# The experts' down product in high and low parts, with all outgoing rows copied by ScalarE

## The chip, the cores and the metric

The kernel runs on one core of one Trainium2 chip. The metric is the device time of one launch in microseconds (us), the median of several runs. The engines named below are TensorE (PE; PEld is its loading of the stationary operand), VectorE (DVE), ScalarE (ACT), GpSimd (POOL), which issues the indirect row moves, and SyncE (SP), which issues the other transfers.

## The reference

Two transformer blocks of 512 rows of 1024 values follow each other, each an attention part and then a layer of experts. The first has 32 experts of which 2 serve each row, the second 64 of which 6 serve each row. For an expert `e` that holds a list of rows `x` with gates `g` it computes, all in float32:

```python
hid = silu(x @ w_gate[e]) * (x @ w_up[e]) * g     # w_gate, w_up: 1024 x 256
out[rows] += hid @ w_down[e]                      # w_down: 256 x 1024
```

One expert's three matrices are 1 MB each.

## The kernel before

`experts_stage` runs once for each block (tags `moe1`, `moe2`). Each engine runs its own program, a loop of steps written out by hand, and semaphores alone set the order between them. Step i holds the gate and up product of expert i and pieces of its neighbours. An expert has one tile of up to 128 rows; experts with longer lists are finished by a later stage that is not changed.

In step i the engines do this, in this order:

- PE: turns `hid` of expert i-1 (2 transposes, L1566); the gate and up product of expert i in four parts of six 512-column matmuls (L1577 to L1579), each part after its own wait; the turns of the gathered rows of expert i+1 (8, L1590), after the gather has landed; the list product of expert i+3 (4 small ones, L1598); the down product of expert i-1 (L1610), four 512-column float32 matmuls, which the trace shows as eight instructions.
- DVE: the low parts of the gate and up weights of expert i+1, parts 0 to 2 (L1620, 128x1024 each); `hid` of expert i (L1633); the low parts of the turned rows of expert i+1 (L1640, twice); part 3 of the weights (L1620); the row numbers of expert i+3 (L1649 and L1651), after the scatter of expert i-3 has landed; the one-hot lists of expert i+4 (L1656); half of the outgoing rows of expert i-1 from PSUM into `ys` (L1664), after the down product.
- ACT: `hidt` of expert i-1 (L1681); the high parts of the weights of expert i+1, parts 0 to 2 (L1673, 128x1024 each); silu of expert i (L1691); the high parts of the turned rows (L1698, twice); part 3 (L1673); the other half of the outgoing rows of expert i-1 (L1706), after the down product and after the scatter of expert i-3 has landed, since `ys` has two buffers.
- POOL: the gather of the rows of expert i+3 (L1723), then the scatter-add of expert i-1 into `acc_dram` (L1733, shown at L1889), which waits until the scatter before it has landed.
- SP: gate and up weights of an expert (L1408) three experts ahead, once a gate and up product has freed the buffer; down weights (L1411) once a down product has.

The gate and up product already works on parts: the high part of a number is its value as fp32r, which ScalarE's copy makes, the low part is what is left, and three fp32r products (high by high, high by low, low by high) take the place of one float32 product. The down product still multiplies `hidt` and the weights in float32.

Of the kernel before, what the change touches and what calls it, by code (L numbers as in the profile page):

```python
# [13 lines left out]
F32 = mybir.dt.float32  # L14
# [3 lines left out]
ALU = mybir.AluOpType  # L18
ACT = mybir.ActivationFunctionType
AX = mybir.AxisListType  # L20

P = 128
# [11 lines left out]
FE = 256  # L34
FH = 2
# [1357 lines left out]
class ExpertWeights:  # L1393


    def __init__(self, K, tag, w_gate, w_up, w_down):
        as_gate_up = lambda a: a.rearrange("p (g c f) -> p g c f", g=2, c=KC)
        self.w_gate, self.w_up, self.w_down = w_gate[0], w_up[0], w_down[0]
        self.gu = [as_gate_up(K.big[:, 4096 * q:4096 * q + 4096]) for q in range(3)]
        self.gu_low = [as_gate_up(K.big_parts[:, 4096 * q:4096 * q + 4096]) for q in range(3)]  # L1400
        self.dn = [K.big[:, 12288 + 2048 * q:14336 + 2048 * q].rearrange("p (j d) -> p j d", j=FH) for q in range(3)]
        self.gu_in = [K.sem(f"{tag}_gate_up{q}_arrived") for q in range(3)]
        self.d_in = [K.sem(f"{tag}_down{q}_arrived") for q in range(3)]
# [106 lines left out]
def experts_stage(K, tag, m, weights, init, next_vectors=None):  # L1510
# [5 lines left out]
    s = K.sem  # L1516
    f = K.heads
    ring2 = lambda a, n: a.rearrange("p (b n) -> p b n", b=2)
    xg, ys = ring2(f[:, 0:2048], 2), ring2(f[:, 4096:6144], 2)
    xt_high, xt_low = ring2(K.heads_parts[:, 2048:4096], 2), ring2(K.heads_parts[:, 8192:10240], 2)  # L1520
    silu, hid, hidt = (ring2(f[:, 6144 + 512 * n:6656 + 512 * n], 2) for n in range(3))
    onehot = f[:, 7680:8192].bitcast(BF16).rearrange("p (b t s) -> p b t s", b=2, t=T)
    idx = K.small[:, 1024:1030].bitcast(I32)
    gate = K.small[:, 1032:1038]
    gu, gu_low, dn, gu_in, d_in = weights.gu, weights.gu_low, weights.dn, weights.gu_in, weights.d_in
    gu_high = K.ht_parts[:, :].rearrange("p (g c f) -> p g c f", g=2, c=KC)
    b_list, b_xt, b_au, b_ht, b_y = K.bank[0], K.bank[1:3], K.bank[3:5], K.bank[5], K.bank[6:8]

# [4 lines left out]
    au_mm, silu_ready, hid_ready = s(f"{tag}_gate_up_product"), s(f"{tag}_silu_ready"), s(f"{tag}_hidden_ready")  # L1533
    ht_mm, ht_copied = s(f"{tag}_hidden_turned"), s(f"{tag}_hidden_turned_copied")
    y_mm, y_dve, y_act = s(f"{tag}_down_product"), s(f"{tag}_y_dve_copied"), s(f"{tag}_y_act_copied")
    cleared = s(f"{tag}_rows_cleared")
# [19 lines left out]
    with nc.Block(no_gpsimd_drain=True) as block:  # L1556
        @block.tensor
        def _(pe):
            def step(i, r, has, fills):
                if has(-1):  # L1560
                    b = (r - 1) % 2
                    pe.wait_ge(hid_ready, i)
                    if late(i, 2):
                        pe.wait_ge(ht_copied, i - 1)
                    for j in range(FH):
                        mm = pe.transpose(b_ht[:, P * j:P * j + P], hid[:, b, j::FH], K.ident[:, :])  # L1566
                    mm.then_inc(ht_mm, 1)
# [33 lines left out]
                if has(-1):  # L1601
                    b, q = (r - 1) % 2, (r - 1) % 3
                    pe.wait_ge(ht_copied, i)
                    pe.wait_ge(d_in[q], fills(-1) * 16)
                    if late(i, 2):
                        pe.wait_ge(y_dve, i - 1)
                        pe.wait_ge(y_act, i - 1)
                    for half in range(2):
                        for j in range(FH):
                            mm = pe.matmul(b_y[half][:, :], hidt[:, b, P * j:P * j + P],  # L1610
                                           dn[q][:, j, 512 * half:512 * half + 512], start=j == 0, stop=j == FH - 1)
                    mm.then_inc(y_mm, 1)
# [3 lines left out]
        def _(dve):  # L1616
# [5 lines left out]

            def step(i, r, has, fills):
                if has(1):
                    for k in range(PARTS - 1):
                        low(i, r, k)
# [25 lines left out]
                if has(4):  # L1652
                    b = r % 2
                    if late(i, -2):
# [3 lines left out]
                                      ALU.is_equal).then_inc(listed, 1)  # L1658
                if has(-1):
                    b = (r - 1) % 2  # L1660
                    dve.wait_ge(y_mm, i)
                    if late(i, 3):
                        dve.wait_ge(scattered, 16 * (i - 2))
                    dve.tensor_copy(ys[:, b, 0:512], b_y[0][:, :]).then_inc(y_dve, 1)  # L1664
            all_steps(dve, step)

        @block.scalar
        def _(act):
# [6 lines left out]
            def step(i, r, has, fills):  # L1675
# [25 lines left out]
                if has(-1):  # L1701
                    b = (r - 1) % 2
                    act.wait_ge(y_mm, i)
                    if late(i, 3):
                        act.wait_ge(scattered, 16 * (i - 2))
                    act.activation(ys[:, b, 512:1024], b_y[1][:, :], ACT.Copy).then_inc(y_act, 1)  # L1706
            all_steps(act, step)

        @block.gpsimd
        def _(pool):  # L1710
# [5 lines left out]
            def step(i, r, has, fills):  # L1716
# [9 lines left out]
                if has(-1):  # L1726
                    b, q = (r - 1) % 2, (r - 1) % 6
                    pool.wait_ge(y_dve, i)
                    pool.wait_ge(y_act, i)
                    if late(i, 2):  # L1730
                        pool.wait_ge(scattered, 16 * (i - 1))
                    pool.sem_inc(row_dmas, 1)
                    scatter_add(K, pool, ys[:, b, :], idx[:, q:q + 1]).then_inc(scattered, 16)  # L1733
# [1093 lines left out]
```

## Time and profile before

| | |
|---|---|
| median of 3 runs | 2048.63 us (2048.20 to 2050.15) |
| the profiled execution | 2047.64 us, its span 2045.9 us |
| experts of block 1 (first gather to last scatter) | 430.8 to 776.1 us |
| experts of block 2 | 1318.1 to 2015.4 us |
| PE busy over the span | 1879.9 us (92%) |
| VectorE, ScalarE, GpSimd busy | 1214.9, 954.0, 612.1 us |

The span runs from the first to the last instruction; the 1.74 us between span and time lie around it. All times in the rows below are counted from the span's start. A busy PE is not a PE at its peak, since the ends of matmuls are modelled and overlap the next ones; the distance from start to start is the better measure there.

### The profile page before, as it was taken

To read this page: it belongs to the slowest core of one execution; us is meant where nothing else is said; L and a number is where in the kernel's file an instruction comes from. 1 tells how busy PE (TensorE), PEld (TensorE's weight loads), DVE (VectorE), ACT (ScalarE), POOL (GpSimd) and SP (SyncE) were. 2 spreads that over 40 slices of the span, in tenths; PEclk is the share of its full clock that TensorE was granted. 3 is DMA by queue.
4 is the path that set the end of the run, shared out by engine and by line. 5 is a ranking of instruction groups with operands and counts; after the bars stand their busy time and mean duration, and the time that the engine had idled before them with its cause. 6 is when DMAs were issued, how large, how long until landed. Compare 5 with 4: busy or idle time off the path is not lost. (4 is left out here: it accounts for less than half of the span.)

```text
span 2045.9 us, 27064 instructions
## 1 busy us (share of the span) xinstructions
PE 1879.9 (92%) x8270; PEld 1292.1 (63%) x8270; DVE 1214.9 (59%) x2232; ACT 954.0 (47%) x1628; POOL 612.1 (30%) x467
## 2 busy tenths in 40 slices
PE   6989988989999995999999969899999999999992
PEld 3434447857777663678678856477666666666661
DVE  1866317367777764661453234577777776776673
ACT  2412227336666554562542222366555655555561
POOL 4997615012322223860200000122222222222221
PEclk9799999989999997999989989999999999999996
DMA  5362410739999864422013264289999999999973
GB/s 185 124 211 87 144 45 26 274 130 330 334 333 330 318 226 149 165 84 83 6 46 120 83 226 165 94 308 340 343 326 325 328 330 337 325 331 324 327 272 104
DMA packets 121435, 441.68 MB, mean 216 GB/s; under 512 B 32037, under 2 KB 36533, under 8 KB 83977
## 3 DMA queue, kind: packets, MB, share of 16 engines
q1 hardware_dynamic: 93672, 406.94, 53.6%
q0 software_dynamic: 27648, 33.67, 7.4%
q8 instruction: 45, 0.74, 0.2%
q14 instruction: 38, 0.30, 0.0%
q10 hardware_dynamic: 32, 0.04, 0.0%
HBM read 446.73 MB, written 63.50 MB: 249 GB/s over the span
## 5 line engine op out<-in xcount | busy, mean ns | idle before, releaser
L1620 DVE TENSOR_TENSOR big_parts<-big,h_cols_parts 128x1024 fp32r<-128x1024 f32 x384 | 460.0, 1223 | 91.7 <-ACT h_cols_parts L1673 83.9
L1673 ACT ACTIVATE h_cols_parts<-big 128x1024 fp32r<-128x1024 f32 x384 | 395.8, 1061 | 62.0 <-PE bank L1579 51.0
L1610 PE MATMUL bank<-big,heads 128*128 128x512 f32 x768 | 352.7, 602 | 1.5 <-ACT heads L1681 1.5
L1889 POOL DMA_INDIRECT acc_scratch<-heads,small x96 | 160.8, 1675 | 606.1 <-DVE small L1651 378.8
L1577 PE MATMUL bank<-h_cols_parts,heads_parts 128*128 128x512 f32 x768 | 309.0, 402 | 4.5 <-DVE heads_parts L1640 4.5
L1579 PE MATMUL bank<-h_cols_parts,heads_parts 128*128 128x512 f32 x768 | 301.1, 392 | 0.0
L1578 PE MATMUL bank<-big_parts,heads_parts 128*128 128x512 f32 x768 | 299.5, 390 | 0.0
L1610 PEld LDWEIGHTS bank<-big,heads 128*128 128x128 f32 x768 | 138.3, 190 | 139.8 <-issue 137.8
L1706 ACT ACTIVATE heads<-bank 128x512 f32<-128x512 f32 x96 | 57.5, 599 | 333.5 <-DMA acc_scratch<-heads,small 263.8
L1577 PEld LDWEIGHTS bank<-h_cols_parts,heads_parts 128*128 128x128 f32 x768 | 145.5, 189 | 31.8 <-DVE heads_parts L1640 5.0
L1723 POOL DMA_INDIRECT heads<-h_scratch,small x96 | 116.2, 1211 | 164.7 <-DVE small L1651 143.8
L1579 PEld LDWEIGHTS bank<-h_cols_parts,heads_parts 128*128 128x128 f32 x768 | 144.4, 188 | 31.6
L1578 PEld LDWEIGHTS bank<-big_parts,heads_parts 128*128 128x128 f32 x768 | 145.0, 189 | 27.6
L458 PE MATMUL bank<-big,h_cols 128*128 128x512 f32 x320 | 143.4, 603 | 0.3 <-ACT heads L608 0.3
L1640 DVE TENSOR_TENSOR heads_parts<-bank,heads_parts 128x512 fp32r<-128x512 f32 x192 | 123.2, 684 | 5.7 <-ACT heads_parts L1698 5.7
L1590 PE MATMUL bank<-ident,heads 128*128 128x128 f32 x768 | 104.8, 279 | 20.4 <-DMA heads<-h_scratch,small 19.9
L1590 PEld LDWEIGHTS bank<-ident,heads 128*128 128x128 f32 x768 | 97.2, 192 | 41.6 <-DMA heads<-h_scratch,small 36.3
L1711 POOL MEMSET heads<- 128x2048 f32 x2 | 3.6, 1807 | 381.6 <-POOLq L1192 381.6
L1698 ACT ACTIVATE heads_parts<-bank 128x512 fp32r<-128x512 f32 x192 | 104.3, 595 | 27.2 <-PE bank L1590 23.9
L1649 DVE TENSOR_SCALAR small<-bank 128x1 int32<-128x1 f32 x96 | 21.3, 222 | 161.1 <-DMA acc_scratch<-heads,small 159.7
L458 PEld LDWEIGHTS bank<-big,h_cols 128*128 128x128 f32 x320 | 60.0, 192 | 76.8 <-issue 76.2
L1113 PE MATMUL bank<-big_parts,x_res_parts 128*128 128x512 f32 x224 | 89.2, 398 | 0.0
(414 smaller groups left out, 3069.1 us busy)
## 6 DMA issues: line engine op xcount, KB each, us to landing
big<-in_w_exp_down_dram SPq DMA_DIRECT2D x96, 1024.0 KB, 13.7
big<-in_w_exp_gate_dram SPq DMA_DIRECT2D x96, 1024.0 KB, 7.2
big<-in_w_exp_up_dram SPq DMA_DIRECT2D x96, 1024.0 KB, 13.8
big<-in_w_in_dram SPq DMA_DIRECT2D x13, 2048.0 KB, 8.9
junk<-in_w_mod_dram SPq DMA_DIRECT2D x12, 1024.0 KB, 5.1
spare<-in_w_mod_dram SPq DMA_DIRECT2D x12, 1024.0 KB, 6.3
big<-in_w_out_dram SPq DMA_DIRECT2D x4, 2048.0 KB, 9.6
h_scratch<-h_rows SPq DMA_DIRECT2D x8, 512.0 KB, 2.6
```

The costliest lines, as they stand in the source:

```text
L458: mm = pe.matmul(out, lhsT, rhs, start=c == 0, stop=c == len(lhs_rhs) - 1)
L1577: pe.matmul(b_au[b][:, :], x_high, gu_high[:, :, c, :], start=c == 0, stop=False)
L1578: pe.matmul(b_au[b][:, :], x_high, gu_low[q][:, :, c, :], start=False, stop=False)
L1579: mm = pe.matmul(b_au[b][:, :], x_low, gu_high[:, :, c, :], start=False, stop=c == KC - 1)
L1590: mm = pe.transpose(b_xt[half][:, P * k:P * k + P], xg[:, b, 4 * half + k::KC], K.ident[:, :])
L1610: mm = pe.matmul(b_y[half][:, :], hidt[:, b, P * j:P * j + P], dn[q][:, j, 512 * half:512 * half + 512], start=j == 0, stop=j == FH - 1)
L1620: dve.tensor_tensor(gu_low[q][:, :, part, :], gu[q][:, :, part, :], gu_high[:, :, part, :].bitcast(F32), ALU.subtract).then_inc(w_low, 1)
L1640: dve.tensor_tensor(xt_low[:, b, part], b_xt[half][:, :], xt_high[:, b, part].bitcast(F32), ALU.subtract).then_inc(xt_low_ready, 1)
L1673: act.activation(gu_high[:, :, part, :], gu[q][:, :, part, :], ACT.Copy).then_inc(w_high, 1)
L1698: act.activation(xt_high[:, b, 512 * half:512 * half + 512], b_xt[half][:, :], ACT.Copy).then_inc(xt_high_ready, 1)
L1723: pool.indirect_dma_start(out=xg[:, b, :], out_offset=None, in_=K.h_dram, in_offset=bass.IndirectOffsetOnAxis(idx[:, q:q + 1], 0), bounds_ ...
L1889: return pool.indirect_dma_start(out=K.acc_dram, out_offset=bass.IndirectOffsetOnAxis(at, 0), in_=rows, in_offset=None, bounds_check=S - 1 ...
```

## The change

The down product is done in fp32r parts as well. ScalarE copies the expert's down weights, two slices of 128x1024, into one buffer `dn_high`; VectorE subtracts and leaves `dn_low` in place of the weights. ScalarE's existing copy of `hidt` now writes its high part, and a new VectorE subtraction of 128x256 makes `hidt_low`. TensorE does twelve fp32r matmuls of 512 columns instead of four float32 ones. VectorE no longer copies outgoing rows; ScalarE copies both halves. The weights of expert i are split at the end of step i, and their product is done in step i+1.

```diff
+    hidt, hidt_low = ring2(K.heads_parts[:, 7168:7680], 2), ring2(K.spare_parts[:, 0:512], 2)
+    dn_high, dn_low = K.junk_parts[:, :].rearrange("p (j d) -> p j d", j=FH), weights.dn_low
 # tensor
-                    pe.wait_ge(ht_copied, i)
-                    pe.wait_ge(d_in[q], fills(-1) * 16)
+                    pe.wait_ge(ht_low_ready, i)
                     if late(i, 2):
-                        pe.wait_ge(y_dve, i - 1)
-                        pe.wait_ge(y_act, i - 1)
-                    for half in range(2):
-                        for j in range(FH):
-                            mm = pe.matmul(b_y[half][:, :], hidt[:, b, P * j:P * j + P],
-                                           dn[q][:, j, 512 * half:512 * half + 512], start=j == 0, stop=j == FH - 1)
+                        pe.wait_ge(y_act, 2 * i - 2)
+                    for j in range(FH):
+                        pe.wait_ge(d_low_ready, 2 * i - 1 + j)
+                        h_high, h_low = (a[:, b, P * j:P * j + P] for a in (hidt, hidt_low))
+                        for half in range(2):
+                            high, low = (a[:, j, 512 * half:512 * half + 512] for a in (dn_high, dn_low[q]))
+                            pe.matmul(b_y[half][:, :], h_high, high, start=j == 0, stop=False)
+                            pe.matmul(b_y[half][:, :], h_high, low, start=False, stop=False)
+                            mm = pe.matmul(b_y[half][:, :], h_low, high, start=False, stop=j == FH - 1)
 # vector, at the start of a step
+                if has(-1):
+                    b = (r - 1) % 2
+                    dve.wait_ge(ht_copied, i)
+                    if late(i, 3):
+                        dve.wait_ge(y_mm, i - 2)
+                    dve.tensor_tensor(hidt_low[:, b, :], b_ht[:, 0:FE], hidt[:, b, :].bitcast(F32),
+                                      ALU.subtract).then_inc(ht_low_ready, 1)
 # vector, at the end of a step
-                if has(-1):
-                    b = (r - 1) % 2
-                    dve.wait_ge(y_mm, i)
-                    if late(i, 3):
-                        dve.wait_ge(scattered, 16 * (i - 2))
-                    dve.tensor_copy(ys[:, b, 0:512], b_y[0][:, :]).then_inc(y_dve, 1)
+                if has(0):
+                    q = r % 3
+                    for j in range(FH):
+                        dve.wait_ge(d_high_ready, 2 * i + (j + 1))
+                        dve.tensor_tensor(dn_low[q][:, j, :], weights.dn[q][:, j, :], dn_high[:, j, :].bitcast(F32),
+                                          ALU.subtract).then_inc(d_low_ready, 1)
 # scalar, at the end of a step
-                    act.activation(ys[:, b, 512:1024], b_y[1][:, :], ACT.Copy).then_inc(y_act, 1)
+                    for half in range(2):
+                        act.activation(ys[:, b, 512 * half:512 * half + 512], b_y[half][:, :], ACT.Copy).then_inc(y_act, 1)
+                if has(0):
+                    q = r % 3
+                    act.wait_ge(d_in[q], fills(0) * 16)
+                    for j in range(FH):
+                        act.activation(dn_high[:, j, :], weights.dn[q][:, j, :], ACT.Copy).then_inc(d_high_ready, 1)
 # gpsimd, before the scatter
-                    pool.wait_ge(y_dve, i)
-                    pool.wait_ge(y_act, i)
+                    pool.wait_ge(y_act, 2 * i)
```

The turns of `hid` (L1566) now wait for `ht_low_ready` of the expert before instead of `ht_copied`. Nothing of SP's program changes.

## Rows read from the trace of the kernel before

**Rows 1.** Busy time by stage: busy us and instructions of each engine, clock, DMA.
```profile
core 0: us, PE busy (x) PEld busy (x) DVE busy (x) ACT busy (x) POOL busy (x), PEclk, DMA share, GB/s
471.68:634.61 162.93, 162.93 (x736) 116.75 (x735) 126.09 (x175) 103.51 (x144) 43.19 (x30) 1.00 0.92 331
...
1356.73:1413.40 56.67, 56.67 (x262) 41.13 (x261) 43.99 (x60) 37.13 (x52) 14.50 (x10) 1.00 0.94 342
1425.00:1987.40 562.40, 544.33 (x2411) 381.87 (x2410) 404.19 (x573) 318.80 (x471) 150.72 (x104) 1.00 0.92 328
```

**Rows 2.** Groups by line, POOL, window 471.68 to 634.61 us.
```profile
L1889 POOL DMA_INDIRECT acc_scratch<-heads,small x15 | 27.6, 1838 | 53.1 <-DMA acc_scratch<-heads,small 41.3 <-DVE small L1651 8.4 <-issue 3.3
```

**Rows 3.** Groups by line, POOL, window 1425 to 1987.4 us.
```profile
L1889 POOL DMA_INDIRECT acc_scratch<-heads,small x52 | 85.6, 1646 | 395.1 <-DVE small L1651 296.9 <-DMA acc_scratch<-heads,small 65.9 <-issue 18.3
```

**Rows 4.** Waits of the whole span: engine, line, releaser, us, times, longest.
```profile
ACT heads L1706 <- DMA acc_scratch<-heads,small: 263.8, 64, 5.4
```

**Rows 5.** Timeline of one step of block 2: start, length, engine, idle before.
```profile
1576.51 0.60 ACT L1706 ACTIVATE heads<-bank 128x512 f32<-128x512 f32 x1 [4.76 <-DMA acc_scratch<-heads,small]
...
1577.36 1.60 POOL L1889 DMA_INDIRECT acc_scratch<-heads,small  x1 [8.07 <-DVE small L1651]
...
1579.27 1.24 POOL L1723 DMA_INDIRECT heads<-h_scratch,small  x1 [0.31 <-issue]
...
1587.41 0.60 ACT L1706 ACTIVATE heads<-bank 128x512 f32<-128x512 f32 x1 [4.99 <-DMA acc_scratch<-heads,small]
...
1588.25 1.61 POOL L1889 DMA_INDIRECT acc_scratch<-heads,small  x1 [7.74 <-DVE small L1651]
```

**Rows 6.** The scatter's line: instruction lengths in ns, and issue to landing.
```profile
L1889 POOL DMA_INDIRECT acc_scratch<-heads,small x96: 1552/1607/2572, 461.4 to 2015.4; - x96
...
DMA to landing us min/median/max: 4.6/10.0/12.6
```

**Rows 7.** The page's DMA issues: queue, count, size, median us to landing.
```profile
big<-in_w_exp_down_dram SPq DMA_DIRECT2D x96, 1024.0 KB, 13.7
...
big<-in_w_exp_up_dram SPq DMA_DIRECT2D x96, 1024.0 KB, 13.8
```

**Rows 8.** Timeline, TensorE in a step in which it never waits.
```profile
1385.59 0.48 PE L1577 MATMUL bank<-h_cols_parts,heads_parts 128*128 128x512 f32 x1
...
1391.14 1.04 PE L1590 MATMUL bank<-ident,heads 128*128 128x128 f32 x8
...
1392.12 3.68 PE L1610 MATMUL bank<-big,heads 128*128 128x512 f32 x8
...
1395.63 0.39 PE L1566 MATMUL bank<-ident,heads 128*128 128x128 f32 x2
1395.78 0.48 PE L1577 MATMUL bank<-h_cols_parts,heads_parts 128*128 128x512 f32 x1
```

**Rows 9.** Timeline, VectorE in the same step.
```profile
1392.21 0.48 DVE L1633 SCALAR_TENSOR_TENSOR heads<-heads,small,bank 128x256 f32<-128x256 f32 x1
1392.60 1.28 DVE L1640 TENSOR_TENSOR heads_parts<-bank,heads_parts 128x512 fp32r<-128x512 f32 x2
...
1395.84 0.69 DVE L1664 COPY heads<-bank 128x512 f32<-128x512 f32 x1
```

**Rows 10.** Timeline, high and low parts of the weights made without a gap.
```profile
1987.32 2.95 ACT L1673 ACTIVATE h_cols_parts<-big 128x1024 fp32r<-128x1024 f32 x3
...
1988.41 3.50 DVE L1620 TENSOR_TENSOR big_parts<-big,h_cols_parts 128x1024 fp32r<-128x1024 f32 x3 [1.15 <-ACT h_cols_parts L1673]
```

**Rows 11.** Timeline, GpSimd and VectorE as the stage of block 2 starts.
```profile
1344.01 0.22 DVE L1649 TENSOR_SCALAR small<-bank 128x1 int32<-128x1 f32 x1
...
1346.47 1.62 POOL L1889 DMA_INDIRECT acc_scratch<-heads,small  x1 [0.30 <-issue]
```

**Rows 12.** Timeline, first and last of the last four scatters of block 2.
```profile
1994.34 1.73 POOL L1889 DMA_INDIRECT acc_scratch<-heads,small  x1 [5.32 <-DMA acc_scratch<-heads,small]
...
2015.40 1.55 POOL L1889 DMA_INDIRECT acc_scratch<-heads,small  x1 [5.51 <-DMA acc_scratch<-heads,small]
```

More of the change, by code:

```diff
@@ L1400, in __init__ @@
         self.gu_low = [as_gate_up(K.big_parts[:, 4096 * q:4096 * q + 4096]) for q in range(3)]
-        self.dn = [K.big[:, 12288 + 2048 * q:14336 + 2048 * q].rearrange("p (j d) -> p j d", j=FH) for q in range(3)]
+        self.dn, self.dn_low = ([a[:, 12288 + 2048 * q:14336 + 2048 * q].rearrange("p (j d) -> p j d", j=FH) for q in range(3)]
+                                for a in (K.big, K.big_parts))
         self.gu_in = [K.sem(f"{tag}_gate_up{q}_arrived") for q in range(3)]
@@ L1520, in experts_stage @@
     xt_high, xt_low = ring2(K.heads_parts[:, 2048:4096], 2), ring2(K.heads_parts[:, 8192:10240], 2)
-    silu, hid, hidt = (ring2(f[:, 6144 + 512 * n:6656 + 512 * n], 2) for n in range(3))
+    silu, hid = (ring2(f[:, 6144 + 512 * n:6656 + 512 * n], 2) for n in range(2))
+    hidt, hidt_low = ring2(K.heads_parts[:, 7168:7680], 2), ring2(K.spare_parts[:, 0:512], 2)
     onehot = f[:, 7680:8192].bitcast(BF16).rearrange("p (b t s) -> p b t s", b=2, t=T)
@@ L1533, in experts_stage @@
     au_mm, silu_ready, hid_ready = s(f"{tag}_gate_up_product"), s(f"{tag}_silu_ready"), s(f"{tag}_hidden_ready")
-    ht_mm, ht_copied = s(f"{tag}_hidden_turned"), s(f"{tag}_hidden_turned_copied")
-    y_mm, y_dve, y_act = s(f"{tag}_down_product"), s(f"{tag}_y_dve_copied"), s(f"{tag}_y_act_copied")
+    ht_mm, ht_copied, ht_low_ready = s(f"{tag}_hidden_turned"), s(f"{tag}_hidden_turned_copied"), s(f"{tag}_hidden_turned_low")
+    d_high_ready, d_low_ready = s(f"{tag}_down_weights_high"), s(f"{tag}_down_weights_low")
+    y_mm, y_act = s(f"{tag}_down_product"), s(f"{tag}_y_copied")
     cleared = s(f"{tag}_rows_cleared")
@@ L1563, in step @@
                     if late(i, 2):
-                        pe.wait_ge(ht_copied, i - 1)
+                        pe.wait_ge(ht_low_ready, i - 1)
                     for j in range(FH):
```

## The prediction

> **What bounds the kernel now.** I read the busy time by stage first. Over long stretches of both expert stages TensorE shows no idle time at all, 162.93 of 162.93 us in block 1 and 56.67 of 56.67 us at the start of block 2, and 544.33 of 562.40 us later on, always at the full granted clock [rows 1]. By this view alone TensorE is the bound, and each us taken from its step would be a us of the kernel. The timeline gives its step where it never waits: 24 gate and up matmuls take 5.55 us from start to start (1385.59 to 1391.14), turns and list 0.98 us, the down product 3.51 us, the turns of `hid` 0.15 us, together 10.19 us [rows 8].
>
> Then I counted the scatters, of which there is one for each expert. From start to start they are 162.93 / 15 = 10.86 us apart in block 1 [rows 1, 2] and 562.40 / 52 = 10.82 us in block 2 [rows 1, 3]. That is slower than TensorE's 10.19 us, in the very stretch in which TensorE never waits. So the scatters fall behind. They may, since `ys` has two buffers; once these are full, ScalarE and VectorE wait for a landing, and TensorE through them. ScalarE's copy of outgoing rows waited for a scatter to land 64 times out of 96, for 263.8 us [rows 4].
>
> One step shows the chain. ScalarE's wait ends when a scatter has landed, at 1576.51. The next scatter starts 0.85 us later, at 1577.36, and its landing releases ScalarE at 1587.41; then the next starts at 1588.25 [rows 5]. Of 10.89 us, 10.05 are one scatter under way. No engine is in this chain except GpSimd for its issue of 1.60 us. A scatter takes so long because the transfers are full: 328 to 342 GB/s at a DMA share of 0.92 to 0.94 [rows 1], and an expert's up weights land 13.8 us after their issue [rows 7], later than the next expert's weights are issued one step of 10.8 us on, so the weights' queue never runs dry. When no weights are left the last scatters are (2015.40 - 1994.34) / 3 = 7.02 us apart [rows 12].
>
> **The change part by part.** TensorE: a down product of twelve fp32r matmuls at the rate of the gate and up product takes 12 / 24 x 5.55 = 2.78 us instead of 3.51, so the step falls from 10.19 to 9.46 us [rows 8]. If TensorE set every step this would be 0.73 x 96 = 70 us. It does not: the scatters' 10.8 us is longer than either.
>
> VectorE: busy now 404.19 / 52 = 7.77 us a step [rows 1]. Two subtractions of 128x1024 come in at 3.50 / 3 = 1.17 us each [rows 10]. The subtraction of 128x256 from PSUM has no row; the pair of 512 columns takes 1.28 us, 0.64 each [rows 9], so it lies between half of that, 0.32, and 0.64; I take 0.40, nearer the half, as length follows columns. The copy of 0.69 us goes [rows 9]. New: 7.77 + 2.34 + 0.40 - 0.69 = 9.82 us. That makes VectorE the busiest engine and is still 1.0 us short of 10.82.
>
> ScalarE: 318.80 / 52 = 6.13 us a step [rows 1], plus two copies at 2.95 / 3 = 0.98 [rows 10] and one at 0.60 [rows 5]: 8.69 us.
>
> The new waits tie the engines to each other. `dn_high` has one buffer, so ScalarE may fill it only after the down product before it (its copies of outgoing rows already wait for that). VectorE waits for ScalarE there, and behind that wait stand `hidt_low`, for which TensorE's next down product waits, and the low parts for the expert after next. The longest loop runs over two steps: the two row copies 1.20, two weight copies 1.96, the second subtraction 1.17, `hidt_low` 0.40, three low parts 3.50, `hid` 0.39 (start to start), the low rows 1.28, 9.90 us in all, then on TensorE 5.55 + 0.98 + 2.78 = 9.31: together 19.21 us, 9.6 us a step [rows 5, 8, 9, 10]. The subtractions start 1.09 us after the copies that take 0.98 us each [rows 10], so a hand-off costs some 0.1 us; with eight of them the loop takes 10.0 us a step. So the engines together need 9.8 to 10.0 us, a little less than the 10.19 of now and clearly less than the scatters' 10.8: the engines' gain stays behind the scatters, and their new load does too.
>
> The waits that move: `d_in` goes from TensorE in step i+1 to ScalarE at the end of step i. Down weights land 13.7 us after issue [rows 7], and the buffer was freed and the load issued over two steps (21.6 us) before, so I count nothing; without that cover it would hold up `hidt` behind it on ScalarE. ScalarE's second row copy makes `ys` ready 0.60 us later; the scatter that takes it starts one whole scatter later, so nothing again. GpSimd's order and SP's program are as before, the bytes moved too.
>
> What is left open to view is the start of a stage, where the scatters have not yet fallen behind. The first scatter of block 2 starts at 1346.47, after the row numbers at 1344.01 [rows 11]. VectorE's added work before that is at most 2.34 + 0.40 = 2.74 us, at least none if it all falls into waits; I take 1.2, less 0.5 for the shorter steps that follow: 0.7 us for each stage, 1.4 in all. At the end of a stage each scatter waits for the one before it [rows 12], and a shorter down product is hidden. Sum, against the profiled execution's own time: 2047.64 + 1.4 = 2049.0 us. That execution lies 1.0 us under the median of 2048.63, which is within what runs differ by. Since 0.2% (4.1 us) is about what a measurement here tells from no change, my forecast is no change, with a range of its own of 2045 to 2053.
>
> **The rivals.** First, TensorE's time counts wherever it never waits. For it: the 219.6 us of full rows, 21.5 steps of 10.19. At VectorE's 9.82 they give 0.37 each, at TensorE's 9.46 0.73: 8 to 16 us, 2032 to 2040. Against it: the scatters in those stretches are no faster (10.86), so being ahead is only waited off later.
>
> Second, the scatters follow the engines: faster steps ask for weights sooner, the transfers take it, and the interval shrinks. The best rate in the rows, 342 GB/s, moves the 328 x 10.82 = 3.55 MB of a step in 10.38 us [rows 1]; 0.44 x 80 steps (the steady ones of both stages) = 35 us, 2013. Were the transfers no limit at all, 10.82 - 9.82 = 1.00 x 80 = 80 us, 1968. Against it: where TensorE ran at 10.19 the scatters stayed at 10.86. The Trainium skill, DMA: Bandwidth & Descriptors, section Specifications, gives some 358 GB/s as one core's share of the memory; by that an estimate of the step would be 3.55 / 358 = 9.9 us and the time some 1975. No row here is above 342 GB/s, so by the trace I give the smaller gain the most of this rival.
>
> Third, slower: VectorE becomes the bound. Its margin falls from 3.0 to 1.0 us a step, and each of its six large subtractions waits for a ScalarE copy just ahead of it. It decides once VectorE loses more than 1.0 us a step to waits, or once the loop's eight hand-offs cost 0.3 us each (9.6 to 10.8). Each 0.1 us beyond costs 8 us over 80 steps; 0.1 to 0.2 give 2057 to 2065. For it: the low parts already waited 1.15 us for ScalarE in a step [rows 10]. Against it: `ys` lets the engines lag nearly a whole step before a scatter starts late.
>
> Fourth, slower in the chain itself: VectorE's added subtractions, both inputs in SBUF, hold up GpSimd's issue of the scatter, which is in the chain. Its length runs from 1.55 to 2.57 us with a median of 1.61 [rows 6]. At 0.2 us more it costs 16 us, 2065; at the longest always, 0.96 x 80 = 77 us, 2126. The Trainium skill, SBUF — State Buffer, section Who interferes with whom, says that such a VectorE instruction contends with a GpSimd instruction that reads SBUF. The median close to the shortest, with four such subtractions a step already there, speaks against much of it here.
>
> **How the numbers follow.** No change 0.47, the first rival 0.16, the second 0.12, the third 0.16, the fourth 0.09. So faster 0.28, same 0.47, slower 0.25. The predicted time is that of the first case, 2049.0. The range takes in the first rival and the third nearly whole, 2030 to 2063; it leaves out the second (0.12) and what of the others lies beyond (some 0.08).
>
> **What would show it.** Right: scatters still some 10.8 us apart in both stages; TensorE's idle time up by about 0.7 us a step, the down product at 2.8 us; VectorE busy about 9.8 us a step; ScalarE still waiting for scatters, but less. Wrong on the fast side: scatters nearer 10.4 with GB/s above 340. Wrong on the slow side: scatters over 10.9 apart with no wait of ScalarE for a landing left, and VectorE idle behind ScalarE's copies; or GpSimd's scatter issue well over 1.65 us.

## The result and the profile after

The changed kernel takes 2056.97 us (median of 7 runs, 2054.2 to 2057.57) where the kernel before took 2050.15 in the same session: a ratio of 1.0031, 95% interval 1.002 to 1.0043. It is slower by 0.31%: some 6.4 us by that ratio, 6.8 between the medians, 7.1 between the two profiled executions. One of the seven runs of the kernel before took 2209.86 us, in a slow state, and is left out of the ratio. The profiled execution took 2054.76 us, its span 2053.0.

First the busy time by stage, in two of the stretches of [rows 1] (columns as there), of the kernel after:

```profile
471.68:634.61 162.93, 158.12 (x811) 131.66 (x810) 154.51 (x209) 134.65 (x195) 49.31 (x31) 1.00 0.92 339
1425.00:1987.40 562.40, 515.93 (x2578) 416.38 (x2577) 498.18 (x668) 429.06 (x620) 159.87 (x104) 1.00 0.90 322
```

TensorE now has idle time in block 1 and 46.5 us of it in block 2; VectorE is busy for 89% of that stretch, ScalarE for 76%. The transfers move 339 and 322 GB/s, where they moved 331 and 328 [rows 1].

The groups by line on GpSimd in the same two stretches answer to [rows 2, 3]:

```profile
L1907 POOL DMA_INDIRECT acc_scratch<-heads,small x15 | 26.4, 1763 | 73.5 <-DMA acc_scratch<-heads,small 42.0 <-DVE small L1664 30.3 <-issue 1.2
...
L1907 POOL DMA_INDIRECT acc_scratch<-heads,small x52 | 87.7, 1687 | 391.8 <-DVE small L1664 254.1 <-DMA acc_scratch<-heads,small 114.2 <-issue 23.5
```

Again 15 and 52 scatters start in these stretches. Such a count can be off by one, so the table below goes from scatter to scatter: 10.69 us apart in block 1 and 10.92 in block 2, where they were 10.78 and 10.82. TensorE's shorter down product has not moved the step. The waits, answering to [rows 4]:

```profile
ACT heads L1720 <- DMA acc_scratch<-heads,small: 188.8, 74, 4.1
DVE big_parts L1676 <- ACT junk_parts L1725: 60.0, 55, 3.9
```

ScalarE still waits for landings, 74 times, but for 188.8 us in place of 263.8. VectorE waits 55 times, for 60.0 us, for the high parts of the down weights.

So I looked for the loss at the ends and the starts of the stages. The timeline of the last steps of block 2, answering to [rows 12], shows one place:

```profile
2007.30 0.39 PE L1615 MATMUL bank<-junk_parts,heads_parts 128*128 128x512 f32 x1
...
2010.04 0.39 PE L1570 MATMUL bank<-ident,heads 128*128 128x128 f32 x2
2010.23 1.09 ACT L1720 ACTIVATE heads<-bank 128x512 f32<-128x512 f32 x2 [2.35 <-PE bank L1617]
2011.21 2.00 ACT L1725 ACTIVATE junk_parts<-big 128x1024 fp32r<-128x1024 f32 x2
2012.30 2.36 DVE L1676 TENSOR_TENSOR big_parts<-big,junk_parts 128x1024 fp32r<-128x1024 f32 x2 [3.90 <-ACT junk_parts L1725]
...
2013.49 2.59 POOL L1907 DMA_INDIRECT acc_scratch<-heads,small  x1 [5.26 <-DMA acc_scratch<-heads,small]
2014.57 0.42 DVE L1635 TENSOR_TENSOR spare_parts<-bank,heads_parts 128x256 fp32r<-128x256 f32 x1
2015.05 0.80 PE L1615 MATMUL bank<-junk_parts,heads_parts 128*128 128x512 f32 x1 [4.62 <-DVE spare_parts L1635]
...
2019.91 0.63 PE L1617 MATMUL bank<-junk_parts,spare_parts 128*128 128x512 f32 x1
2020.57 1.09 ACT L1720 ACTIVATE heads<-bank 128x512 f32<-128x512 f32 x2 [7.09 <-PE bank L1617]
2022.52 1.55 POOL L1907 DMA_INDIRECT acc_scratch<-heads,small  x1 [6.44 <-ACT heads L1720]
```

The down product of the last expert but one takes 2.74 us from start to start (2007.30 to 2010.04). Only when it is done may ScalarE fill `dn_high` for the last expert, since that buffer is the only one: row copies, high parts, low parts, `hidt_low`, one behind the other. TensorE waits 4.62 us for them. Then its twelve matmuls take some 5.25 us, as the granted clock has fallen to the lower of its two levels:

```profile
2010.00:2015.05 5.05, 0.43 (x4) 0.20 (x2) 2.69 (x3) 3.25 (x5) 1.56 (x1) 0.90 0.13 24
2015.05:2020.30 5.25, 5.25 (x12) 3.79 (x12) 0.00 (x0) 0.00 (x0) 1.03 (x1) 0.50 0.51 76
```

Those are windows of the kernel after, with the columns of [rows 1]; 0.50 is 1.2 GHz of 2.4, after a stretch in which TensorE was busy for 0.43 us. The last scatter therefore waits for ScalarE's copy and not for the scatter before it. It comes 9.03 us after that one, where the last three intervals of before were 7.02 on average [rows 12]. Block 1 ends in the same way: TensorE waits 4.62 us, and its last matmuls start 0.43 us apart at first and 0.23 at the end.

The other place is the start of block 2. GpSimd and VectorE there, in the timeline of the kernel after, from the first scatter to the third:

```profile
1343.72 2.59 POOL L1907 DMA_INDIRECT acc_scratch<-heads,small  x1 [0.30 <-issue]
...
1352.00 2.34 DVE L1676 TENSOR_TENSOR big_parts<-big,junk_parts 128x1024 fp32r<-128x1024 f32 x2
1352.36 2.92 POOL L1742 DMA_INDIRECT heads<-h_scratch,small  x1 [6.05 <-DMA acc_scratch<-heads,small]
...
1354.61 3.48 DVE L1626 TENSOR_TENSOR big_parts<-big,h_cols_parts 128x1024 fp32r<-128x1024 f32 x3
1355.58 3.98 POOL L1907 DMA_INDIRECT acc_scratch<-heads,small  x1 [0.30 <-issue]
...
1369.45 1.58 POOL L1907 DMA_INDIRECT acc_scratch<-heads,small  x1 [6.54 <-issue]
```

and GpSimd in the kernel before, following the scatter of [rows 11]:

```profile
1355.37 1.05 POOL L1723 DMA_INDIRECT heads<-h_scratch,small  x1 [7.28 <-DVE small L1651]
1356.73 1.60 POOL L1889 DMA_INDIRECT acc_scratch<-heads,small  x1 [0.30 <-issue]
...
1370.26 1.69 POOL L1889 DMA_INDIRECT acc_scratch<-heads,small  x1 [3.68 <-DMA acc_scratch<-heads,small]
```

Beside VectorE's subtractions of down weights and gate and up weights, the gather's issue takes 2.92 us instead of 1.05 and the next scatter's 3.98 instead of 1.60. The first two intervals come to 25.73 us (1343.72 to 1369.45) instead of 23.79. Over the whole kernel after, 89 of the 96 gathers begin while VectorE makes one of its 128x1024 subtractions, and these take 1.45 us on average, the longest 2.92; the seven others take 0.99 to 1.52.

### The profile page after: what moved, and what is told of

The parts are those of the page before. It is cut to its first block and busy times, and to the rows that moved or that the text cites. A ratio compares the mean times of both kernels' runs of the same rounds, so it can differ in the third digit from the quotient of the medians.

```text
span 2053.0 us, 28332 instructions
## 1 busy us (share of the span) xinstructions
PE 1839.3 (90%) x8654; PEld 1367.1 (67%) x8654; DVE 1391.9 (68%) x2424; ACT 1156.6 (56%) x1916; POOL 637.9 (31%) x467
## 5 line engine op out<-in xcount | busy, mean ns | idle before, releaser
L1626 DVE TENSOR_TENSOR big_parts<-big,h_cols_parts 128x1024 fp32r<-128x1024 f32 x384 | 451.6, 1216 | 4.1 <-ACT h_cols_parts L1686 3.3
L1686 ACT ACTIVATE h_cols_parts<-big 128x1024 fp32r<-128x1024 f32 x384 | 389.4, 1071 | 17.1 <-PEq L1192 8.9
L1907 POOL DMA_INDIRECT acc_scratch<-heads,small x96 | 167.4, 1744 | 634.3 <-DVE small L1664 345.8
L1582 PE MATMUL bank<-big_parts,heads_parts 128*128 128x512 f32 x768 | 300.8, 392 | 0.0
L1676 DVE TENSOR_TENSOR big_parts<-big,junk_parts 128x1024 fp32r<-128x1024 f32 x192 | 226.9, 1223 | 75.5 <-ACT junk_parts L1725 60.0
L1720 ACT ACTIVATE heads<-bank 128x512 f32<-128x512 f32 x192 | 104.4, 596 | 228.5 <-DMA acc_scratch<-heads,small 188.8
L1725 ACT ACTIVATE junk_parts<-big 128x1024 fp32r<-128x1024 f32 x192 | 192.9, 1061 | 0.0
L1742 POOL DMA_INDIRECT heads<-h_scratch,small x96 | 137.4, 1432 | 123.0 <-DVE small L1664 92.8
L1615 PE MATMUL bank<-junk_parts,heads_parts 128*128 128x512 f32 x384 | 159.7, 416 | 10.4 <-DVE spare_parts L1635 10.2
L1617 PE MATMUL bank<-junk_parts,spare_parts 128*128 128x512 f32 x384 | 151.7, 395 | 0.0
L1616 PE MATMUL bank<-big_parts,heads_parts 128*128 128x512 f32 x384 | 151.3, 394 | 0.0
```

The source lines that it names most:

```text
L1582: pe.matmul(b_au[b][:, :], x_high, gu_low[q][:, :, c, :], start=False, stop=False)
L1615: pe.matmul(b_y[half][:, :], h_high, high, start=j == 0, stop=False)
L1616: pe.matmul(b_y[half][:, :], h_high, low, start=False, stop=False)
L1617: mm = pe.matmul(b_y[half][:, :], h_low, high, start=False, stop=j == FH - 1)
L1626: dve.tensor_tensor(gu_low[q][:, :, part, :], gu[q][:, :, part, :], gu_high[:, :, part, :].bitcast(F32), ALU.subtract).then_inc(w_low, 1)
L1676: dve.tensor_tensor(dn_low[q][:, j, :], weights.dn[q][:, j, :], dn_high[:, j, :].bitcast(F32), ALU.subtract).then_inc(d_low_ready, 1)
```

## The experiments

Theory A: full transfers and the chain of scatters set the step, and the loss lies at the ends of the stages. B: ScalarE's second row copy makes it. C: VectorE has become the bound. D: it is spread over all steps. E: VectorE's added subtractions stretch GpSimd's issues. F and G: something other than the transfers, or the transfers without the chain, sets 10.8 us.

The table collects all runs. "Intervals" are worked out from the scatters' starts in each run's one profile: the first two of block 2 together; the mean from the third to the sixth from the end, in block 1 and block 2; the last of each block. The mean gather and scatter are the lengths of their issues on GpSimd. Each ratio is to the kernel before on the same chip.

| run | median us (before) | ratio, 95% | gather, scatter mean ns | first two | steady | last |
|---|---|---|---|---|---|---|
| before, profile | | | 1211, 1675 | 23.79 | 10.78, 10.82 | 6.26, 7.06 |
| after, profile | | | 1432, 1744 | 25.73 | 10.69, 10.92 | 9.46, 9.03 |
| e1 | 2048.01 (2049.32) | 0.9996, 0.9983 to 1.0009 | 1302, 1652 | 22.56 | 10.77, 10.84 | 5.84, 6.62 |
| e2 | 2057.58 (2049.32) | 1.0039, 1.0023 to 1.0054 | 1868, 1763 | 26.91 | 10.77, 10.87 | 9.86, 8.40 |
| e3 | 2046.89 (2049.32) | 0.9990, 0.9977 to 1.0003 | 1575, 1803 | 26.28 | 10.67, 10.83 | 5.73, 6.57 |
| e4 | 2048.40 (2049.32) | 0.9997, 0.9984 to 1.0011 | 1060, 1671 | 23.85 | 10.77, 10.89 | 8.40, 8.42 |
| e5 | 2010.76 (2050.39) | 0.9811, 0.9794 to 0.9828 | 1059, 1594 | 20.42 | 10.22, 10.22 | 5.97, 6.65 |
| e6 | 1974.14 (2050.39) | 0.9628, 0.9612 to 0.9645 | 1653, 1915 | 24.33 | 9.78, 9.76 | 10.33, 9.45 |
| e7 | 2080.43 (2050.39) | 1.0149, 1.0131 to 1.0167 | 1038, 1589 | 20.41 | 10.30, 10.65 | 4.66, 4.75 |
| e8 | 2081.37 (2050.39) | 1.0148, 1.0118 to 1.0178 | 2620, 2328 | 19.10 | 10.45, 10.77 | 4.92, 4.93 |
| e9 | 2058.52 (2049.50) | 1.0041, 1.0024 to 1.0059 | 1737, 1994 | 26.17 | 10.88, 10.88 | 6.19, 6.86 |
| e10 | 2056.32 (2049.50) | 1.0030, 1.0016 to 1.0043 | 1633, 1731 | 21.87 | 10.83, 10.99 | 5.95, 6.81 |
| e11 | 2057.44 (2049.50) | 1.0033, 1.0019 to 1.0047 | 1461, 1750 | 26.24 | 10.78, 10.81 | 10.34, 8.38 |
| e12 | 2044.31 (2049.09) | 0.9981, 0.9965 to 0.9996 | 1476, 1797 | 22.08 | 10.72, 10.92 | 5.81, 6.60 |

**e1 and e2: the row copies.** e1 is the kernel before with ScalarE copying both halves, e2 the kernel after with VectorE copying one half again. Of the edit of e1, the two copies (the waits that go with them are left out here; e2 is its opposite):

```diff
 # vector
-                    dve.tensor_copy(ys[:, b, 0:512], b_y[0][:, :]).then_inc(y_dve, 1)
 # scalar
-                    act.activation(ys[:, b, 512:1024], b_y[1][:, :], ACT.Copy).then_inc(y_act, 1)
+                    for half in range(2):
+                        act.activation(ys[:, b, 512 * half:512 * half + 512], b_y[half][:, :], ACT.Copy).then_inc(y_act, 1)
```

> The kernel before with one part of the change alone: ScalarE copies both halves of the outgoing rows, VectorE none; the down product stays as it was. Theory A (scatters set the step, the loss of the whole change lies at the starts and ends of the expert stages, in the splitting of the down weights): within 0.2% of the kernel before, some 2048 to 2052 us, scatters 10.8 us apart in both stages, the last interval of a stage longer by one copy at most, 0.6 us. Theory B (the loss comes from ScalarE, which now holds each scatter back by a second copy): slower by the 5 to 7 us that the whole change lost, 2054 to 2057 us, with the intervals 0.1 us longer.

> The kernel after with VectorE copying one half of the outgoing rows again; the split down product stays. Theory A: as slow as the kernel after less one copy at each stage's end, 2055 to 2058 us; VectorE's busy time rises by 0.69 us a step to some 10.3 us and the scatter interval stays under 11. Theory B (ScalarE's second copy makes the loss): back to within 0.2% of the kernel before, 2047 to 2052 us. Theory C (VectorE is close enough to the bound to set the step): 0.3 to 0.7 us more a step over 80 steps, 2070 us or more.

e1 is as fast as the kernel before, e2 as slow as the kernel after. B falls: who copies the rows makes no difference beyond the 2.7 to 3.2 us that these intervals leave open either way, and the loss comes with the split down product. C falls for the steady part too, since e2 keeps VectorE busy 0.6 us a step longer (529.93 us in place of 498.18 from 1425 to 1987.4) and the intervals stay.

**e3: a second buffer for the high parts.** ScalarE splits the weights ahead of the row copies; the buffer lies in `h_rows`, which the stage does not use. Of the edit, ScalarE's new block; the old one behind the row copies goes, and TensorE and VectorE read the buffers in turn:

```diff
+                if has(0):
+                    q = r % 3
+                    act.wait_ge(d_in[q], fills(0) * 16)
+                    if late(i, 2):
+                        act.wait_ge(y_mm, i - 1)
+                    for j in range(FH):
+                        act.activation(dn_high[r % 2][:, j, :], weights.dn[q][:, j, :], ACT.Copy).then_inc(d_high_ready, 1)
                 if has(-1):
                     b = (r - 1) % 2
                     act.wait_ge(y_mm, i)
```

> The kernel after with a second buffer for the high parts of the down weights, so that ScalarE splits an expert's down weights before it copies the rows of the expert before, not behind them. Theory A: the last interval between scatters of a stage falls from 9.0 and 9.5 us to 6.5 to 7.2 us, 4 to 6 us in all, and the start of block 2 gives back up to 2 us: 2049 to 2053 us, not to be told from the kernel before; the steady interval stays at 10.7 to 10.9. Theory D (the loss is spread over all steps, by VectorE or GpSimd): 2055 to 2058 us, as the kernel after.

The loss is gone: a ratio of 0.9990 where the kernel after has 1.0031 and 1.0033. That is some 8.4 us, and the time lies under the 2049 to 2053 that A expected. The end of block 2 in its timeline:

```profile
1997.72 2.00 ACT L1721 ACTIVATE h_rows_parts<-big 128x1024 fp32r<-128x1024 f32 x2
...
2002.04 0.50 PE L1616 MATMUL bank<-h_rows_parts,heads_parts 128*128 128x512 f32 x1 [1.68 <-DVE spare_parts L1636]
...
2004.67 0.39 PE L1618 MATMUL bank<-h_rows_parts,spare_parts 128*128 128x512 f32 x1
...
2006.48 1.55 POOL L1910 DMA_INDIRECT acc_scratch<-heads,small  x1 [5.03 <-ACT heads L1728]
2013.05 1.55 POOL L1910 DMA_INDIRECT acc_scratch<-heads,small  x1 [5.02 <-DMA acc_scratch<-heads,small]
```

The split now runs beside the product before it; TensorE waits 1.68 us instead of 4.62 and keeps the higher clock (1.00 from 2002.04 to 2005.00 us), and the last scatter waits for its predecessor again. The two last intervals are 6.2 us shorter than after's, which is most of the 8.4; the rest is within the intervals of the ratios. The start of block 2 gave nothing back (26.28), so that part of the expectation failed; the start has another cause.

**e4 and e9: VectorE's two subtractions alone.** e4 takes them out of the kernel after (TensorE multiplies by the high parts in place of the low ones); e9 puts two such subtractions into the kernel before, on data that nobody waits for. The edits in part; e4's change on TensorE is left out:

```diff
 # e4, vector
-                    for j in range(FH):
-                        dve.wait_ge(d_high_ready, 2 * i + (j + 1))
-                        dve.tensor_tensor(dn_low[q][:, j, :], weights.dn[q][:, j, :], dn_high[:, j, :].bitcast(F32),
-                                          ALU.subtract).then_inc(d_low_ready, 1)
 # e9, vector, at the end of a step, ahead of the row copy
+                    for j in range(FH):
+                        if late(i, 1):
+                            dve.wait_ge(more, 2 * i - 1 + j)
+                        dve.tensor_tensor(K.junk_parts[:, 1024 * j:1024 * j + 1024], K.hr[:, j, :], K.hr[:, j + 2, :],
+                                          ALU.subtract).then_inc(more, 1)
```

> The kernel after without VectorE's two subtractions that make the low parts of the down weights; TensorE multiplies with the high parts in their place, so the count of its matmuls stays (the low part of the down weights is left out of the result). Theory A: the last down product of a stage no longer waits for the subtractions, 1 to 2 us at each stage's end, 2053 to 2056 us, steady intervals still 10.7 to 10.9. Theory E (the fourth rival: VectorE's added subtractions stretch GpSimd's issue, which is in the chain of scatters): the mean length of a scatter on GpSimd falls from 1744 back to some 1675 ns, the steady intervals by 0.07 us, 6 us over 80 steps, and with the ends 2046 to 2050 us.

> The kernel before with two subtractions of 128x1024 from SBUF more at the end of each VectorE step, whose result nothing reads; no engine waits for them. VectorE's busy time rises by 2.34 us a step, as by the low parts of the down weights. Theory E (they stretch GpSimd's issue of gathers and scatters, which counts where no landing is waited for, at the start of a stage): the mean gather rises from 1211 to some 1400 ns, the first two intervals of block 2 from 23.8 to some 26 us together, the end of a stage stays as before; 2051 to 2056 us. Theory A (all of the loss lies in the split that the last down product waits for): no change, 2047 to 2052 us, first two intervals of block 2 23 to 24 us.

e4 takes the loss away as well. e9 makes more than the whole of it (1.0041) with no down product changed, and more than the 2051 to 2056 us that E expected. GpSimd at the start of block 2 in e4:

```profile
1352.15 1.05 POOL L1736 DMA_INDIRECT heads<-h_scratch,small  x1 [7.56 <-DMA acc_scratch<-heads,small]
1353.50 1.59 POOL L1901 DMA_INDIRECT acc_scratch<-heads,small  x1 [0.30 <-issue]
...
1366.81 2.04 POOL L1901 DMA_INDIRECT acc_scratch<-heads,small  x1 [4.11 <-issue]
```

and in e9:

```profile
1348.81 2.86 POOL L1729 DMA_INDIRECT heads<-h_scratch,small  x1 [7.48 <-DVE small L1651]
1352.32 3.98 POOL L1895 DMA_INDIRECT acc_scratch<-heads,small  x1 [0.65 <-issue]
1358.62 2.91 POOL L1729 DMA_INDIRECT heads<-h_scratch,small  x1 [2.32 <-DVE small L1651]
```

Without the subtractions the gather takes 1.05 and the scatter 1.59 us, with them 2.9 and 3.98. That is E, at the start of a stage. In e4 only 2 of the 96 gathers begin while a subtraction of VectorE runs, in e9 92. Part of what E expected of e4 did not come: the steady intervals did not shrink. Of its 7 us against the kernel after, the last intervals hold 1.7, the first two of block 2 1.9 and those of block 1 0.9 (21.12 less 20.24); some 2.5 are not located, which is no more than its interval leaves open. In e9 VectorE's row numbers and its row copy also come later, so its 8.4 us are not GpSimd's alone: the first two intervals of block 2 hold 2.4 of them, and what the steady ones add (10.88 in both blocks) is no more than two profiles of one kernel differ by (e11).

**e5 and e6: most of the down weights not loaded.** From the fourth expert on only 128 of 1024 columns are loaded, in the kernel before (e5) and after (e6, in which the split reads other data of the same shape).

```diff
-        sp.dma_start(self.dn[q], self.w_down[expert1(e)].rearrange("e (p j) d -> (e p) j d", p=P)).then_inc(self.d_in[q], 16)
+        part = slice(0, D if isinstance(e, int) and e < 3 else 128)
+        sp.dma_start(self.dn[q][:, :, part], self.w_down[expert1(e)].rearrange("e (p j) d -> (e p) j d", p=P)[:, :, part]).then_inc(self.d_in[q], 16)
```

> The kernel before with the loads of the down weights cut to 128 of 1024 columns from the fourth expert on (the rest of the buffer keeps older weights, so the result of the down products is another). All waits, instructions and engines' work stay; 0.92 of some 3.55 MB a step are no longer moved. Theory A (full transfers make the scatters slow, and these set the step): the scatter interval falls from 10.8 us to TensorE's own step, 10.2 to 10.3 us, about 0.55 x 80 = 44 us less, some 2005 us, and ScalarE's waits for landings go. Rival F (something else than the transfers sets 10.8, an order of waits among the engines): the interval stays at 10.7 or above, 2040 us or more.

> The kernel after with the same cut of the loads; the down weights that ScalarE and VectorE split are other data of the same shape, so the result is another, the instructions are the same. Theory A with the step loop of the prediction: the scatter interval falls below that of the kernel before with the same cut, to 9.6 to 10.0 us, so this kernel is 15 to 45 us faster than the other, 1960 to 1990 us; the gain of TensorE's shorter step then shows once the transfers no longer cover it. Rival C (VectorE and its hand-offs with ScalarE take more than the loop's 10.0 us): interval of 10.4 us or more, slower than the kernel before with the same cut.

The clearest pair. The busy time from 1425 to 1930 us, of e5:

```profile
1425.00:1930.00 505.00, 505.00 (x2269) 361.36 (x2268) 392.18 (x547) 319.02 (x445) 129.98 (x99) 1.00 0.77 257
```

and of e6:

```profile
1425.00:1930.00 505.00, 503.45 (x2574) 419.79 (x2573) 492.60 (x664) 429.07 (x617) 187.92 (x102) 1.00 0.79 259
```

From the scatter's line in e5:

```profile
DMA to landing us min/median/max: 4.0/5.6/9.1
```

With room in the transfers (257 GB/s) a scatter lands 5.6 us after its issue in place of 10.0 [rows 6], TensorE never waits in e5, and the scatters are 10.22 us apart: TensorE's step of [rows 8]. In e6 they are 9.77 apart, within the 9.6 to 10.0 of the loop; VectorE is busy for 98% of that stretch, so the loop and VectorE's own work are not told apart there. The change is then worth 2010.76 - 1974.14 = 36.6 us, 0.45 x 80. F and C fall.

**e7 and e8: two accumulators.** Scatters of even and odd experts go to two accumulators; e7 is the kernel before, e8 that of e3. Of the edit, the scatter; the other waits for a landing follow, and the zeroing and adding of the second accumulator are left out here.

```diff
-                    if late(i, 2):
-                        pool.wait_ge(scattered, 16 * (i - 1))
-                    scatter_add(K, pool, ys[:, b, :], idx[:, q:q + 1]).then_inc(scattered, 16)
+                    if late(i, 3):
+                        pool.wait_ge(*landed(i - 3, r + 1))
+                    scatter_add(K, pool, ys[:, b, :], idx[:, q:q + 1], (K.acc_dram, K.acc_odd[tag])[b]).then_inc(scattered[b], 16)
```

> The kernel before with scatters of even and odd experts into two accumulators, so that a scatter waits for the one two before it; the odd one is zeroed at the start of a stage and added at its end, which costs some 4 and 6 MB of transfers a stage, 30 to 40 us in all. Theory A (the chain from scatter to scatter sets the step): the interval falls to what the transfers allow, 10.2 to 10.4 us, and 80 steps give 32 to 48 us back: 2035 to 2055 us. Rival G (the transfers alone set it, and the chain only follows): the interval stays at 10.75 to 10.85 and the time is 2075 to 2090 us.

> The kernel after with the second buffer for high parts and the two accumulators. Theory A: the interval falls to the limit of the transfers, 10.0 to 10.4 us, below that of the kernel before with two accumulators if TensorE's 10.2 us had held that one; 2020 to 2050 us. Rival G: 10.75 to 10.85 us and 2070 to 2090 us.

Both theories had a part in the interval; the time is the one that G expected. In e7 the interval falls to 10.30 in block 1, nearly TensorE's step, and in block 2 only to 10.65, with the transfers at 332 GB/s and a DMA share of 0.93 (from 1425 to 1987.4 us). So the chain costs some 0.2 to 0.5 us of the step, and the full transfers hold the rest. e8 gains less (10.45 and 10.77), for which no cause is shown; its gathers take 2.62 us on average and its scatters 2.33, against 1.04 and 1.59 in e7. Zeroing and adding the second accumulator cost more than the steps gave, so neither is of use.

**e10 and e12: the row numbers ahead of the subtractions.** Both start from e3. VectorE makes the row numbers (L1662, L1664), which release the gather, ahead of the low rows instead of behind the last low part: in every step in e10 (`if has(3)`), in the steps before the fifth expert's in e12, whose edit this is.

```diff
+                if has(3) and not late(i, 4):
...
+                    dve.tensor_reduce(gate[:, q:q + 1], b_list[:, 2:5], AX.X, ALU.add).then_inc(idx_ready, 1)
                 if has(1):
                     b = (r + 1) % 2
                     for half in range(2):
```

> The kernel after with the second buffer for high parts, and VectorE makes the row numbers ahead of the low rows and the last low part, not behind them, so that a gather is issued some 3 us earlier, ahead of the subtractions of the down weights. Theory E: the first two intervals of block 2 fall from 26.3 to 24 us or less, and with the stage ends as in the kernel with the second buffer alone the time is 2042 to 2046 us. Rival: the row numbers wait for a landing, and earlier in VectorE's order that wait holds up the low rows and through them TensorE: 2048 us or more, with waits of VectorE for landings of some 100 us.

> The kernel after with the second buffer for high parts, and the row numbers made early only in the steps before the fifth expert's, where no landing is waited for yet; after that in the old order. Theory E with the stage ends mended: gathers of 1.0 us at the start of block 2 in place of up to 2.9, its first two intervals 22 to 24 us together in place of 26.3, steady intervals 10.8, last intervals 5.7 to 7.0; 2041 to 2046 us, faster than the kernel before by 0.2 to 0.4%. Rival (what is won at the start is waited off behind the full transfers): the first two intervals shorten, the stage does not, 2046 to 2050 us.

e10 shortens the start (21.87) and loses it in the steps (10.83 and 10.99). Its waits show scatters held up by ScalarE's row copies:

```profile
POOL acc_scratch L1910 <- ACT heads L1728: 85.3, 14, 8.8
```

That is 14 times, where e3 has one wait of 5.0 us. VectorE's waits for landings are 90.6 us against 86.4 in e3, so the rival's reason is not shown; why the engines fell behind stays open. e12 keeps the old order in the later steps and has the lowest ratio of the kernels that leave nothing out: 0.9981, interval 0.9965 to 0.9996, 4.8 us under the kernel before. GpSimd at its start of block 2:

```profile
1342.70 1.05 POOL L1754 DMA_INDIRECT heads<-h_scratch,small  x1 [3.72 <-DVE small L1657]
1345.60 2.89 POOL L1919 DMA_INDIRECT acc_scratch<-heads,small  x1 [1.85 <-ACT heads L1737]
...
1358.16 3.58 POOL L1919 DMA_INDIRECT acc_scratch<-heads,small  x1 [4.91 <-DMA acc_scratch<-heads,small]
```

The gather is out of the way before the scatter wants GpSimd; the scatters themselves are still stretched. The first two intervals are 4.2 us shorter than in e3. But from the first scatter of block 2 to the last, e12 takes 672.1 us (1336.08 to 2008.22) and e3 671.6 (1341.42 to 2013.05), and the intervals of the two ratios overlap. So the rival, that what is won at the start is waited off later, is not ruled out, and that e12 is faster than e3 is not shown.

**e11: the kernel after once more.**

> The kernel after once more, unchanged, for the spread of one profile: 2054 to 2059 us; last intervals of the stages 9.0 to 9.5 us and first two of block 2 some 26 us together by either theory; the steady intervals of block 2, 10.92 in the first profile, anywhere in 10.8 to 10.95.

Time, starts and steady intervals are as expected. The last intervals are 10.34 and 8.38 us, not 9.0 to 9.5 each; their sum is 18.7, and it was 18.5 the first time. The steady interval of block 2 is 10.81 this time and 10.92 the first, so no cause is needed for the 0.1 us by which the first profile differs from before.

## Why the prediction was right in the main and 8 us off

The forecast of no change came with a range of its own, 2045 to 2053 us, and the median of 2056.97 lies outside it. It lies within 2030 to 2063 only because the third rival widened that range, by a mechanism that did not come about; so much of it was luck.

**What bounds the kernel: right.** Scatters stayed 10.69 and 10.92 us apart (10.78 and 10.82 before) while TensorE's step shrank; with lighter transfers the step became TensorE's 10.2 us at once (e5). Chain and transfers both hold it (e7).

**The prices: right.** The down product takes 2.74 us (2.78 predicted). VectorE is busy 498.18 / 52 = 9.58 us a step (9.82), ScalarE 429.06 / 52 = 8.25 (8.69). The loop of 9.6 to 10.0 us was measured bare at 9.77 (e6). TensorE's idle time rose by (46.47 - 18.07) / 52 = 0.55 us a step (0.7).

**The end of a stage: the step that failed.** The prediction said that there "each scatter waits for the one before it [rows 12], and a shorter down product is hidden". It had named the mechanism itself, one `dn_high` buffer that may be filled only after the product before, and priced it in the steady loop alone, where 10.8 less 10.0 us leave 0.8 of cover. In the last step there is no cover: TensorE waits 4.62 us and then runs at the lower clock, and the last intervals grow by 9.46 - 6.26 + 9.03 - 7.06 = 5.2 us. It counted 0. e3 shortened this wait to 1.68 us, at the higher clock, and the loss went with it.

**The start of a stage: mis-sized.** 0.7 us each was counted. Block 1 came to 21.12 - 20.43 = 0.7 us in its first two intervals, block 2 to 1.9, and to 2.4 in e11. The bound of 2.74 took VectorE's own time; the trace shows GpSimd's issues stretched beside it. Together 5.2 + 0.7 + 1.9 = 7.8 us, against 7.1 between the two profiled executions. In this pair that fits in part by chance: the steady intervals of block 2 add 5.7 us, and the rest of the span gives 6.4 back. In e11, whose steady intervals are those of before, the same ends and starts come to 5.4 + 0.6 + 2.4 = 8.4 us, and its span is 8.2 us longer than before's.

**The rivals.** The first (TensorE's time counts) and the second (the scatters follow the engines) fell. The third gave a range, 2057 to 2065, at whose lower end the time came out, but VectorE is not what sets 10.8 us (e2, e6). The fourth had the right mechanism in the wrong place: VectorE's subtractions do hold up GpSimd's issue (e4, e9), yet in the steady stretch of block 2 the mean scatter grew only from 1646 to 1687 ns [rows 3], 0.04 x 52 = 2 us; the price falls at the start, where no landing is waited for. The rule of the Trainium skill that stood with it (SBUF — State Buffer, Who interferes with whom: a VectorE instruction with two SBUF inputs contends with GpSimd's reads of SBUF) agrees with e4 and e9: the mean gather is 1060 ns without the added subtractions and 1432 with them, 1211 against 1737 in the kernel before.

**Open:** some 2.5 us of what e4 gave back, most of what e9 lost, why e10 loses in the steps, and whether the earlier row numbers of e12 gain anything.

## What to carry to other kernels

When work moves off the engine that seems busiest and a chain of transfers sets the step, price the change where that chain does not cover it: the first and the last steps of the stage. A single buffer that costs nothing inside the loop can put a whole split, and a TensorE that has fallen to its lower clock, behind the last product; here a second buffer took a loss of 0.31% away (ratio 0.9990). With the row numbers ahead of the subtractions as well the ratio was 0.9981; that the order added to it is not shown. Taking part of the load off the suspected bound (e5 and e6) shows in one pair what the engines alone would need.

## What was not expected of the hardware

- At the start of block 2, issues of indirect transfers on GpSimd took 1.05 us (gather) and 1.59 (scatter) where no 128x1024 subtraction of VectorE ran as they began (e4), and 2.92 and 3.98 us where one did, in the kernel after. Not each one is stretched: the gather at 1342.42 in the kernel after took 0.99 us while one ran.
- At the end of block 2, after 4.62 us without work, TensorE's granted clock was 0.50 for the next 5.25 us, so that twelve matmuls cost 5.25 us instead of 2.74.
- A scatter-add landed 10.0 us after its issue (median) beside weights at 328 to 342 GB/s, and 5.6 us after it at 257 GB/s (e5).
